# Moving eighteen small parameter loads one weight piece earlier, and one modulation step behind a projection step, in a hybrid attention / RWKV / HGRN / mixture-of-experts layer

## The reference, cut to what matters

```
mod  = silu(c) @ w_mod + b_mod              # 6 x 1024 columns: shift1 scale1 gate1 shift2 scale2 gate2
h    = rms_norm(x) * (1 + scale1) + shift1
proj = h @ w_in                             # 3200 columns, split among three mixers
mix  = concat(attention, rwkv7, hgrn2)      # small parameters: rw_w0, rw_a0, rw_w2, rw_a2, rw_g2, hg_lb, ...
x    = x + gate1 * (mix @ w_out)
h2   = rms_norm(x) * (1 + scale2) + shift2
x    = x + gate2 * moe(h2)                  # top 4 of 32 experts
y    = rms_norm(x)
```

## Time and profile before

| what | value |
|---|---|
| median of 3 runs | 1302.47 us (1298.92 to 1303.51) |
| profiled execution | 1299.72 us, span 1298.0 us |
| PE busy | 1182.1 us, 91% of the span |
| DVE, ACT, POOL busy | 313.2, 228.2, 39.4 us |
| moved by DMA | 459.94 MB, 354 GB/s over the span |
| chain that ended last | DMA 53%, PE 39%, DVE 4%, ACT 2% |

### The profile page before, as it was taken

One profiled execution on the slowest core, in us unless ns is written; L12 is line 12 of the kernel. 1 busy time (PEld: TensorE's weight loads), 2 busy tenths in 40 slices (PEclk: granted clock), 3 DMA queues, 4 the chain that ended last, 5 costly groups with the idle time before them and its releaser, 6 DMA issues.

```text
span 1298.0 us, 17311 instructions
## 1 busy us (share of the span) xinstructions
PE 1182.1 (91%) x7132; PEld 475.2 (37%) x7132; DVE 313.2 (24%) x632; ACT 228.2 (18%) x381; POOL 39.4 (3%) x70
## 2 busy tenths in 40 slices
PE   4989998887999999999999999999999999999994
PEld 1435587663433333333333333332333333333231
DVE  1204567643212111111211111111121111111113
ACT  2112255523111111111111111111111111111112
POOL 0300100000000000000000000000000000000000
PEclk9999999998899999999999999999999999999997
DMA  9898001069099999999999999999999999999991
GB/s 373 285 372 342 6 3 61 17 246 406 26 426 429 428 428 428 428 428 428 427 427 428 428 428 427 428 428 428 426 429 428 428 427 428 428 428 428 428 428 57
DMA packets 44241, 459.94 MB, mean 354 GB/s; under 512 B 5112, under 2 KB 7328, under 8 KB 16432
## 3 DMA queue, kind: packets, MB, share of 16 engines
q1 hardware_dynamic: 41152, 451.98, 82.9%
q0 software_dynamic: 2576, 6.35, 1.7%
q10 hardware_dynamic: 480, 1.13, 0.2%
HBM read 457.96 MB, written 1.47 MB: 354 GB/s over the span
## 4 chain that ended last, share of the span: by engine, by line
DMA 53%; PE 39%; DVE 4%; ACT 2%; issue 1%; DVEq 0%; SPq 0%; ACTq 0%
DMA ring<-in_moe_w_gu_dram 47%; PE bank L1177 16%; PE bank L575 5%; PE bank L1197 4%; DMA ring<-in_w_mod_dram 3%; DMA ring<-in_w_in_dram 1%; DMA proj<-in_norm_ffn_g_dram 1%; PE bank L689 1%; PE bank L550 1%; PE bank L1140 1%; PE bank L1155 1%; PE bank L563 1%; PE bank L1167 1%; PE bank L1099 1%; DMA const_sb<-in_constants_dram 1%
## 5 line engine op out<-in xcount | busy, mean ns | idle before, releaser
L1177 PE MATMUL bank<-ring,proj 128*64 128x512 f32 x2048 | 459.6, 599 | 32.9 <-DMA ring<-in_moe_w_gu_dram 32.6
L1177 PEld LDWEIGHTS bank<-ring,proj 128*64 128x64 f32 x2048 | 140.6, 137 | 350.4 <-issue 275.8
L1197 PE MATMUL bank<-ring,proj 128*64 128x512 f32 x1024 | 233.8, 598 | 11.9 <-DVE proj L2073 11.9
L2064 DVE TENSOR_SCALAR proj<-bank 128x512 f32<-128x512 f32 x32 | 22.1, 692 | 481.3 <-PE bank L1177 481.3
L1540 ACT ACTIVATE proj<-proj 128x512 f32<-128x512 f32 x32 | 20.2, 630 | 605.1 <-DVE proj L2064 605.1
L1197 PEld LDWEIGHTS bank<-ring,proj 128*64 128x64 f32 x1024 | 69.0, 136 | 131.9 <-issue 131.9
L575 PE MATMUL bank<-ring,hT 128*128 128x512 f32 (+2 forms) x224 | 88.6, 551 | 0.2 <-DMA ring<-in_w_in_dram 0.2
L2076 DVE COPY proj<-bank 128x512 f32<-128x512 f32 x32 | 22.1, 691 | 249.1 <-PE bank L1197 249.1
L1155 PE MATMUL bank<-proj 64*128 64x512 f32 x256 | 63.6, 615 | 0.0
L1140 PE MATMUL bank<-h_nat,proj 128*64 128x512 f32 x264 | 62.3, 593 | 0.0
L575 PEld LDWEIGHTS bank<-ring,hT 128*128 128x128 f32 x224 | 41.7, 190 | 44.7 <-issue 39.0
(11 more groups left out here) (332 smaller groups left out, 793.5 us busy)
## 6 DMA issues: line engine op xcount, KB each, us to landing
ring<-in_moe_w_gu_dram SPq DMA_DIRECT2D x128, 2048.0 KB, 24.4
ring<-in_moe_w_down_dram SPq DMA_DIRECT2D x64, 2048.0 KB, 21.7
ring<-in_w_mod_dram SPq DMA_DIRECT2D x12, 2048.0 KB, 15.6
ring<-in_w_in_dram SPq DMA_DIRECT2D x5, 2048.0 KB, 17.3
ring<-in_w_out_dram SPq DMA_DIRECT2D x2, 2048.0 KB, 8.4
const_sb<-in_constants_dram POOLq DMA_DIRECT2D x1, 2450.0 KB, 13.0
ring<-in_w_in_dram SPq DMA_DIRECT2D x1, 1536.0 KB, 9.6
ring<-in_w_in_dram SPq DMA_DIRECT2D x1, 1024.0 KB, 13.6
```

The source lines that it names most:

```text
L1177: mm = pe.matmul(b[CAP * half:CAP * half + CAP, :], xT[:, k % 4, k // 4, :], ring[:, j, 2048 * kc + o + 512 * half:2048 * kc + o + 512 * h ...
L1197: mm = pe.matmul(b_down[CAP * half:CAP * half + CAP, :], aT[:, k % 4, k // 4, :], ring[:, 4 + j, D * kc + 512 * half:D * kc + 512 * half + ...
L2064: ts(moe["glu"], bank[4][:, :], LIMIT, None, ALU.min).then_inc(sem("glu_sb"), 1)
```

## The change

Two edits. On POOL, the wait for "in" 2 is taken out, so the eighteen small requests stand directly behind that of `kk`. On PE, `modulation("mod", 2)` and `project(3, 0)` change places. Everything else is the same; since two lines are gone, line numbers behind them are two lower in the changed kernel.

```diff
@@ -460,8 +460,6 @@
             slot, times = FRONT_AT["in", 1]
             pool.wait_ge(ring_full[slot], 16 * times)
             pool.dma_start(Pm("kk"), a["rw_kk"][0].unsqueeze(0).to_broadcast([P, 256])).then_inc(sem("kk_in"), 16)
-            slot, times = FRONT_AT["in", 2]
-            pool.wait_ge(ring_full[slot], 16 * times)
             for name, src in (
@@ -991,8 +989,8 @@
             project(2, 0)
             modulation("mod", 1)
             project(2, 1)
+            project(3, 0)
             modulation("mod", 2)
-            project(3, 0)
             rw_lora(0)
             modulation("mod", 3)
             project(3, 1)
```

## The result

| | median, us | lowest to highest | runs |
|---|---|---|---|
| before | 1301.03 | 1298.92 to 1303.51 | 4 |
| changed | 1291.84 | 1290.88 to 1297.39 | 4 |

Ratio 0.9941, 95% interval 0.9914 to 0.9967. Two later measurements of the same changed kernel gave 0.9964 (0.9951 to 0.9978) and 0.9945 (0.9926 to 0.9963). The two medians of the table alone give 0.9929, inside the first interval.

What follows compares the result with a forecast made beforehand. DMA transfers up to "mod" 6 were taken as the bound: it lands 2.7 us earlier, less 1.35 for a slow step, about 1.4 us gained from 1301.2, giving 1299.8 us, range 1293.8 to 1303.8.

Steps and rivals of the forecast that it cites:

- part 1: Small loads requested directly behind `kk`: ring pieces land 4.3 us earlier, which alone removes the 5.59 us wait at "mod" 2.
- the hole: DMA engines nearly idle from 42.0 to 47.1 us, share 0.03; filling it was to give 4.3 us.
- the small loads' cost: The eighteen small loads' transfers were taken to cost 11.1 us of all 16 DMA engines.
- the clock's charge: Slow PE step behind the 2.6 us wait at "mod" 6, charged at 1.35 us, between 0 and 1.7.
- What is lost again up to "mod" 4: Of 4.3 us gained, some 2.3 were to be left when "mod" 4 lands, up to 3.0 by work alone.
- The new hole: DMA idle time of 1.0 to 1.5 us, expected between "in" 4 landing at 87.1 and the constants starting at 88.5.
- more than 4.5 us: Sign of being wrong: "mod" 6's step starting that much earlier would mean the DMA engines were not the bound.
- The wait at `project(2, 0)`: PE was to wait 1.2 us there for "in" 2, out of 0, 1.2 or 2.9 us.
- the rule of the Trainium skill: DMA engines alternate between queues, one packet each; "in" 2 lands at 60.9 and "mod" 4 at 98.8, both in time.
- Case D: Nothing gained: "in" 2 takes 18.4 us, PE waits 2.9 us and runs slow; 1300.2 us, chance 0.18.
- Case C: Slower: constants starve "mod" 4, which takes 16.2 us and lands at 104.2; 1302.8 us, chance 0.15.
- Case B: Whole wait gained, 6.0 to 7.2 us, with "mod" 6 there when PE comes; 1294.0 us, chance 0.17.

Runs made afterwards that it cites:

- before_again: No edit: the kernel before, profiled and timed once more; median 1301.92 us.
- after_again: No edit: the changed kernel, profiled and timed once more; ratio to the kernel before 0.9964, median 1294.18 us.
- loads_at_in2: Changed kernel, but POOL requests the small loads only when `project(0, 1)` is done, as SP requests "in" 2; ratio to the kernel before 1.0013.
- router_busy: Changed kernel with six more filler products on PE ahead of the second norm's transposes, in the router's stage; ratio to the kernel before 0.9946.
- loads_only: Kernel before with only the POOL edit, small loads behind `kk`, PE's order as before; ratio to the kernel before 0.9947.
- const_in3: Changed kernel with constants and router's weight requested when "in" 3 has landed instead of "mod" 3; ratio to the kernel before 0.9959.
- after: First profiled measurement of the changed kernel, no further edit; ratio to the kernel before 0.9941, median 1291.84 us.

## Why the prediction was wrong

The mechanism was right: the small loads' part sets the time, part 1 takes the wait at "mod" 2 away alone, and the chain of transfers up to "mod" 6 bounds the gain. That the swap adds nothing fits it too, since the forecast counted it only as cover. The steps that failed are the sizes of three terms of the sum: the hole, what is kept of it behind (with the small loads' cost taken as fixed), and the clock's charge. The pair with equal starts at 33.5 us shows them; the pair with equal starts at 32.3 us, which is set out behind them, shows how far they hang on the start.

**The hole, forecast 4.3 us, was 6.3.** The stretch 42.0 to 48.8 us in `before_again` and `after_again`:

```profile
42.00:48.80 6.80, 6.80 (x17) 3.04 (x16) 1.18 (x3) 0.00 (x0) 0.00 (x0) 1.00 0.06 19
```
```profile
42.00:48.80 6.80, 6.80 (x17) 3.04 (x16) 1.24 (x3) 0.00 (x0) 6.80 (x12) 1.00 0.99 206
```

(0.99 - 0.06) x 6.8 = 6.3 us. I had two numbers wrong. The lag of 3.9 us from request to start, which I took from the old place, is no fixed lag: "mod" 1 still held the DMA engines there. At the new place `w0` is requested at 38.53 and the DMA engines are full from 42.0 on, with no gap between the transfers of the two queues. And the hole ends when SP requests "in" 2, which hangs on PE, and so on the clock of the first 36 us. I read it from one profile with an early start, where SP requests at 46.28 us; in `before_again` it is 47.50, 1.2 us later. In the stretch 42.0 to 48.8 us the DMA engines are idle for (1 - 0.21) x 6.8 = 5.4 us in the first and (1 - 0.06) x 6.8 = 6.4 us in the second. The hole's far end moves from run to run, and its near end does not.

**The cost of the small loads, taken as fixed, fell in this pair.** q0's share of 57.4 to 76.0 us in `before_again`, and of 41.0 to 57.4 us in `after_again`:

```profile
q0 software_dynamic: 864, 2.21, 64.9%
```
```profile
q0 software_dynamic: 912, 2.34, 63.4%
```

That is 12.1 us before, and 10.4 us after, of which about 0.3 are `kk`, whose share of 4.3% over 8 us lay outside the first stretch. With the hole this makes 6.3 + 2.0 = 8.3, and "in" 4 did land 8.0 us earlier (79.07 + 13.3 = 92.4 against 79.02 + 5.3 = 84.3), where I had 4.3. But this sum is not shown to be the reason. In `loads_at_in2` q0's share of 46 to 78 us is 30.5%, 9.8 us, as low as in the hole, and "in" 4 landed no earlier; and with early starts it is 39.8% of 28 us = 11.1 us in the first profile of before (50 to 78 us) and 32.6% of 36 us = 11.7 us in `router_busy` (42 to 78 us), no fall at all. What makes 8.0 us out of a hole of 6.3 stays open.

**What is lost again up to "mod" 4, forecast 2.0, was 1.2.** That piece landed 6.8 us earlier (88.31 + 15.6 = 103.9 against 87.77 + 9.3 = 97.1). The new hole that I had put between "in" 4 and "mod" 4 is not there in this pair: from 84 to 90 us the DMA share is 0.96 in `after_again`. (My "up to 3.0 by work alone" was off as well: 102.95 - 99.6 is 3.4.) Another one has opened, ahead of "in" 4, which SP requests at 79.02 when `project(2, 1)` is done; the transfers are now so early that they wait for PE here:

```profile
79.00:82.00 3.00, 3.00 (x8) 1.33 (x8) 0.69 (x1) 0.00 (x0) 0.34 (x1) 1.00 0.63 205
```

`loads_only` has it too (0.74), so it is not the swap's.

**The clock's charge, forecast 1.35, was 0 in this pair.** The wait ahead of "mod" 6 was 1.26 us, not 2.6, and the step behind it took 1.92. So it was in four profiles (waits of 1.25, 1.26, 1.26 and 1.02 us); the slow step came only where the wait was 2.54 or 2.95. So the gain at "mod" 6 was 6.7 us instead of 2.7 - 1.35. I had written that more than 4.5 us here would mean that the DMA engines were not the bound. That sign was wrong with the size of the hole: PE still waits for `w_mod` at this step.

**The same terms with an early start.** The first profile of before and `router_busy` start at 32.25 and 32.41 us, which is the start that I had worked from. The stretch 42.0 to 48.8 us, before and changed:

```profile
42.00:48.80 6.80, 6.80 (x17) 2.98 (x16) 2.30 (x6) 0.00 (x0) 0.00 (x0) 1.00 0.21 53
```
```profile
42.00:48.80 6.80, 6.80 (x17) 3.00 (x16) 2.18 (x5) 0.00 (x0) 6.80 (x13) 1.00 0.96 184
```

Here the hole gives (0.96 - 0.21) x 6.8 = 5.1 us. "in" 4 lands 5.3 us earlier (91.45 against 78.01 + 8.1 = 86.1). A new hole is there, with a DMA share of 0.08 from 84 to 85 us, and "mod" 4 lands 3.8 us earlier (102.95 against 86.76 + 12.4 = 99.2). "mod" 6's step starts 3.8 us earlier and takes 1.5 us more. That leaves 2.3 us, and SP's first expert request moves by as much (278.48 against 276.15). The forecast had 1.35. So for the start that it was worked out from, the forecast was 1 us too low at "mod" 6; in the pair that starts later it was 5.3 us too low (6.7 against 1.35). These are two pairs of single profiles. How often each start comes among the runs that were not profiled is not known, so the 5 to 8 us of the ratios can't be added up from them.

**The other points.** The wait at `project(2, 0)`, 1.2 us in the forecast, did not come: "in" 2 took 13.5 us in `after_again` and landed at 60.9, 2 us ahead of PE. With the early start of `router_busy` it took 15.1 and landed at 61.5, 0.4 us ahead of PE. The first is the lower of my bounds (60.8 by work alone) and also what the rule of the Trainium skill (DMA: Bandwidth & Descriptors, Queues, rings and completion order) gave (60.9); the landing cannot tell the two apart. The queues do not agree with the rule at first: from 48.8 to 51.0 us of `after_again` q0 has 87.1% and q1, on which "in" 2 was requested at 47.45, has 0.5%, while alone, in `before_again`, q1 has 90.0% there. From 51 to 54 us they roughly do (42.0 to 60.7%). Case D rested on one row from a more crowded place. Case C did not occur: "mod" 4 took 9.3 and 12.4 us in the two changed profiles, not 16.2. Case B had the right size for the later start, 6.0 to 7.2, but not its reason, since "mod" 6 was still waited for. I gave it 0.17 because I held a hole of 5.1 us against it, a number of one profile. That the shift passes one to one to the end is right as far as single profiles show it: 6.7 at "mod" 6, 6.6 at the first expert request, and 951 us from the first expert product on for both. The stretch between these two varies by 3.5 us by itself.

## What to carry to other kernels

When transfers bound a stage, look first for the time in which the DMA engines have nothing to do, and put small loads there; taking them out of a crowded stretch without filling an idle one gained nothing here. A wait that one reorders away may only uncover the next one on the same chain: a row with 0.27 us of idle time ahead of it held 6 us. And before a hole or a lag is used as a bound, ask what sets each of its ends; where one end hangs on something that changes between executions, one profile is not enough.

## What the runs showed of the hardware

- The granted clock differed between executions of the same code in the first 36 us and at 317 to 334 us. The first projection step started anywhere from 32.25 to 35.77 us; the later stretch cost 3.5 us or not. By an estimate from these figures, together they can make most of the 5.1 to 6.5 us between the fastest and the slowest run of the changed kernel.
- After idle times of 1.0 to 1.3 us ahead of "mod" 6 the next step took 1.92 us; after 2.54 and 2.95 us it took 3.44 and 3.47. Ahead of "mod" 3 in `const_in3`, 1.97 us of idle time were followed by a step of 2.83 us.
- A 2 MB piece beside the small loads took 10.0 us where they were requested 11 us ahead of it (`after`), 13.5 us where 9 us ahead (`after_again`), 15.1 us where 7 us ahead (`router_busy`; it landed between 60.0 and 61.5 us in all three), 15.4 us where both were requested at the same moment (`loads_at_in2`), and 18.4 us where they were requested 6 us ahead of it but began late, behind another large piece. Alone it took 7.7.
